# Activations as the loaded weights: FFNs, output projections and cross output of a three-layer block in f32 products, with the residual stream turned to tokens on the partitions

## Chip, cores and metric

One core of one Trainium2 chip. Times are device microseconds of a whole execution; lower is better. A matmul here has a stationary operand (128x128, put in by an instruction of its own, the weight load) and a moving operand, whose columns stream through.

## What is computed

x is 256 tokens by 2048 features, all in f32. Two layers:

```python
h = rms_norm(x, norm1_g[l])
q, k, v, gu, gv = split(h @ w_in[l])            # 2048 x 3584
attn = banded_window_attention(rope(norm(q)), rope(norm(k)), v, sink)
sgu  = chunked_spatial_gating(gelu(gu), gelu(gv), ...)
x = x + concat(rms_norm(attn), rms_norm(sgu)) @ w_o[l]        # 2048 x 2048
a = depthwise_conv(rms_norm(x) @ w_up[l])       # 2048 x 11264, three taps along the tokens
x = x + (silu(a_gate) * a_up) @ w_down[l]       # 5632 x 2048
```

Then one layer of another kind: a mixer of dilated attention and a state-space scan (input 2048 x 6160, output `w_out` 2048 x 2048), cross attention to 256 memory tokens (`w_ckv`, `w_cq`, and the output `w_co`, 512 x 2048), and an FFN `relu(h @ w_up)**2 @ w_down` with 8192 hidden features. Each part reads an rms norm of x and adds to x.

## The kernel before

All weight matrices are cut into 560 pieces of 1 MB (128 partitions x 2048 numbers) in the order of use. For each piece SP issues the load into one of four slots `w_raw`, as soon as TensorE has finished the piece four before (`acc_done`); ACT rounds it to the format fp32r (`w_hi`, L1031), DVE subtracts (`w_lo`, L1462, in place of `w_raw`), both two pieces ahead of TensorE (`tick(p, s)` splits piece p + 2). Every product is three fp32r matmuls: hi x hi, hi x lo, lo x hi. ACT, DVE and TensorE each run the pieces in the written order, with their other work placed between `tick`s by hand; a later operation waits for all before it on its engine.

Features lie on the partitions everywhere. The residual stream `xs` is [16 chunks of 128 features, 256 tokens]. Weights are the stationary operand, activations move, 256 columns (tokens) at a time, 48 matmuls a piece. `wide` makes 128 output features from all 2048 inputs (L456 to L458), `deep` 512 output features from 512 inputs (L473 to L475), `mixed_half` one half of an output projection (L516 to L518), because the two halves have their own rms factor and the factors are applied after the product, per column (token), by DVE (`add_mixed`). `evac_scaled` takes a finished bank out of PSUM times the token factor (L1491), `evac_deep` adds a down piece to `xs` (L1497, two additions of 128x512).

An FFN block of the layers is 8 up pieces (512 gate and 512 up features) and the 4 down pieces of the block before. For each pair of up pieces: ACT makes the base of the convolution (L1206), DVE adds two taps (L1695, L1696), ACT the silu (L1210), DVE the product (L1714), ACT `h_hi` (L1212), DVE `h_lo` (L1716). A loop runs over five pairs of blocks. The second FFN has 16 blocks of 4 up and 4 down pieces.

The inputs of a projection are x times the norm's gain, split in hi (ACT, L1034) and lo (DVE, L1479); the rms factor comes later. Its sum of squares: POOL squares x in eight steps and sums (L360, L362), TensorE sums over the partitions with a matrix of ones (`total_pairs`, L489), ACT and DVE make the inverse root over 128x256 (`inverse_root`). At the start x comes in one transposed load of four parts, `wdt` (the 16 step columns of the mixer) with the constants; DVE waits for the constants ahead of w_lo of piece 2.

Of the kernel before, what the change touches and what calls it, by code (L numbers as in the profile page):

```python
# [15 lines left out]
P = 128  # L40
# [62 lines left out]
LAYER_LINKS = 159  # L103
NORMS = 7
SQUARED, SUMMED = 24, 20
# [3 lines left out]
def build(nc, x, weights, wdt, params1, params2, consts, consts1, w_s, b_s, mem, positions, out):  # L109
    ctx = ExitStack()  # L110
    with ctx:
# [16 lines left out]
        xs = fixed("x_stream", [KC, T])  # L128
# [20 lines left out]
        wdt_sb = fixed("wdt_sb", [KC, SSM_HEADS])  # L149
# [13 lines left out]
        ff = at("ff_tmp", [6, T], F32, AA)  # L163
        gr, ur, ga, ua, gs, hm = (ff[:, i] for i in range(6))
# [22 lines left out]
        sums2 = at("factored", [2, T], F32, AA + 8 * KB)  # L187
# [20 lines left out]
        sq_x = at("sq_x", [KC, T], F32, AR + 16 * KB)  # L208
# [22 lines left out]
        def psb(a, n):  # L231
# [19 lines left out]
        first_squares = sem("first_squares")  # L251
# [30 lines left out]
        wdt_ready, dt_sums, softplus_in, softplus_out, dt_rows = (  # L282
            sem(n) for n in ("wdt_ready", "dt_sums", "softplus_in", "softplus_out", "dt_rows"))
# [35 lines left out]
        @block.sync  # L319
        def _(sp):  # L320
            x_parts = x.rearrange("(c p) t -> p c t", p=P)
            for s in range(W_SLOTS):
                if s == 1:
                    for j in range(4):
                        sp.dma_start(xs[:, 4 * j:4 * j + 4], x_parts[:, 4 * j:4 * j + 4]).then_inc(x_in[j], 16)
                sp.dma_start(w_raw[:, s], weights[s]).then_inc(raw_in[s], 16)
            with sp.Fori(1, PIECES // W_SLOTS) as i:
# [6 lines left out]
            y = out.rearrange("(c p) t -> p c t", p=P)  # L334
            for j in range(DOWN):
                sp.wait_ge(acc_free, PIECES - DOWN + j + 1 + 4)
                sp.dma_start(y[:, 4 * j:4 * j + 4], xs[:, 4 * j:4 * j + 4]).then_inc(out_done, 16)
            sp.wait_ge(out_done, 16 * DOWN)
# [3 lines left out]
        def _(pool):  # L342
# [5 lines left out]
            pool.dma_start(wdt_sb[:], wdt).then_inc(consts_in, 16)  # L348
# [17 lines left out]
            for i in range(7):  # L366
                pool.wait_ge(first_squares, (i + 1) // 2 + 1)
                if i:
                    pool.wait_ge(x_summed, i)
                G.tensor_tensor(sqa[:], sqa[:] if i else sq_x[:, 0:2], sq_x[:, 2 * i + 2:2 * i + 4],  # L370
                                ALU.add).then_inc(x_summed, 1)
            pool.wait_ge(consts_in, 4 * 16)
            with pool.Fori(0, LAYERS) as l:
                P0, N0, SQ0, SU0 = l * LAYER_PIECES, l * NORMS, l * SQUARED, l * SUMMED + 7

                pool.wait_ge(acc_free, P0 + 4)
# [4 lines left out]
                pool.wait_ge(sums_ready, N0 + 3)  # L381
# [16 lines left out]
                for i in range(4):  # L398
                    pool.wait_ge(gated, 2 * l + (1 if i < 3 else 2))
                    add_squares(SQ0 + 4, SU0 + 3, i, proj[:, U1 + 2 * i:U1 + 2 * i + 2], N0 + 4)  # L400

                for i in range(8):
                    pool.wait_ge(acc_free, P0 + P_OUT + (2 * i + 2 + 4))
                    add_squares(SQ0 + 8, SU0 + 6, i, xs[:, 2 * i:2 * i + 2], N0 + 5)

                for i in range(8):
                    pool.wait_ge(acc_free, P0 + (LAYER_PIECES - DOWN + i // 2 + 1 + 4))
                    add_squares(SQ0 + 16, SU0 + 13, i, xs[:, 2 * i:2 * i + 2], N0 + 6)
            N0, SQ0, SU0 = LAYERS * NORMS, LAYERS * SQUARED, LAYERS * SUMMED + 7

            pool.wait_ge(acc_free, P_IN2 + 4)
            pool.dma_start(pos_sb[:], positions.to_broadcast([P, T])).then_inc(positions_in, 16)
            pool.wait_ge(gains_ready, 2 * LAYERS + 2)
            pool.wait_ge(sums_ready, N0 + 3)
# [3 lines left out]
            for n in range(4):  # L418
                pool.wait_ge(heads_copied, LAYERS * 2 + n + 1)
                add_squares(SQ0, SU0, n, proj[:, Q2 + 2 * n:Q2 + 2 * n + 2], N0)  # L420
# [9 lines left out]
            for i in range(8):  # L430
                add_squares(SQ0 + 4, SU0 + 3, i, mem_sb[:, 2 * i:2 * i + 2], N0 + 3)
            pool.wait_ge(acc_free, 4 + P_KV)
            for i in range(8):
                add_squares(SQ0 + 12, SU0 + 10, i, xs[:, 2 * i:2 * i + 2], N0 + 5)
            for i in range(8):
                pool.wait_ge(acc_free, P_CO + i // 2 + 1 + 4)
                add_squares(SQ0 + 20, SU0 + 17, i, xs[:, 2 * i:2 * i + 2], N0 + 6)
# [3 lines left out]
        def _(pe):  # L441
# [4 lines left out]
            def wide(p, s, acts, free=1, ready=None):  # L446
# [3 lines left out]
                pe.wait_ge(acc_free, p + free)  # L450
                o = ps[:, s, 0:T]
                for c in range(KC):
# [6 lines left out]
                last.then_inc(acc_done, 1)  # L459


            FREE = (3, 2, 2, 1)

            def deep(p, s, hi_in, lo_in):
# [11 lines left out]
                last.then_inc(acc_done, 1)  # L476
# [14 lines left out]

            def per_head(n, o, sq, chunks, per_row=1, base=K_SEL):
# [11 lines left out]
            def mixed_half(p, s, half, ready=None):  # L504

                if half == 0:
                    pe.wait_ge(w_ready, p + 1)
                    pe.wait_ge(acc_free, p + 1)
                o = ps[:, s, half * T:(half + 1) * T]
                src_hi, src_lo = (act_hi, act_lo) if half else (mix_hi, mix_lo)  # L510
                for i in range(8):
                    c = 8 * half + i
                    hi, lo = w_hi[:, s, c * P:(c + 1) * P], w_lo[:, s, c * P:(c + 1) * P]
                    if ready is not None:
                        pe.wait_ge(act_ready, ready + c + 1)
                    mm(o, hi, src_hi[:, i], start=i == 0, stop=False)  # L516
                    mm(o, hi, src_lo[:, i], start=False, stop=False)  # L517
                    last = mm(o, lo, src_hi[:, i], start=False, stop=i == 7)  # L518
                if half:
                    last.then_inc(acc_done, 1)  # L520
# [38 lines left out]
            with pe.Fori(0, LAYERS) as l:  # L559
                P0, N0, S0, A0, SU0 = l * LAYER_PIECES, l * NORMS, l * 2, l * PREPS, l * SUMMED + 7  # L560

# [1670 lines left out]
```

## Time and profile before

| what | value |
|---|---|
| median of 3 runs | 3573.75 us (3571.2 to 3575.15) |
| the profiled execution, first to last instruction | 3573.6 us |
| TensorE matmuls | 3485.6 us busy, 27974 records |
| TensorE weight loads | 3415.4 us busy, 27974 |
| DVE, ACT, POOL busy | 2339.1, 1532.4, 284.6 us |
| read from memory | 594.54 MB, 167 GB/s over the span |
| mean granted clock of TensorE | 0.983 |

Matmuls overlap, so a busy TensorE is not one at its peak: the distance between starts says more than the busy time. A plain f32 matmul leaves two records, an fp32r matmul or a transpose one. The profiled execution has only its span (3573.6); it lies at the median of the runs.

### The profile page before, as it was taken

How to read it: one execution, taken by the hardware profiler on the slowest of the kernel's cores; microseconds unless marked ns; L12 is line 12 of the kernel's file. 1: busy time of each engine (PE TensorE's matmuls, PEld its weight loads, DVE VectorE, ACT ScalarE, POOL GpSimd, SP SyncE). 2: the span in 40 equal slices, each digit the busy share in tenths (PEclk: the TensorE clock that was granted, in tenths of full speed). 3: DMA queues.
4: the chain of work that ended last, by engine and by line, in shares of the span. 5: the costliest groups of instructions: out<-in, count | busy, mean ns of one | idle time of the engine just before them, and what ended most of it. 6: DMA issues, size and time to landing. Idle time of an engine off the chain costs nothing.

```text
span 3573.6 us, 67331 instructions
## 1 busy us (share of the span) xinstructions
PE 3485.6 (98%) x27974; PEld 3415.4 (96%) x27974; DVE 2339.1 (65%) x2609; ACT 1532.4 (43%) x1578; POOL 284.6 (8%) x177
## 2 busy tenths in 40 slices
PE   8999999999999999999999999999999899999999
PEld 8999999999998989999999999989898899999999
DVE  5658666666667658766666668467777756555555
ACT  4554434443443454444344344337643433333332
POOL 1113000000003013000000002010032200000000
PEclk9999999999999999999999999999999999999999
DMA  6335545555554424545454454433354355554544
GB/s 225 131 112 182 181 177 182 174 187 177 177 179 160 152 107 175 179 179 177 176 187 175 181 177 156 165 129 136 126 184 146 130 178 187 177 187 177 187 177 165
DMA packets 86527, 600.05 MB, mean 168 GB/s; under 512 B 9328, under 2 KB 13456, under 8 KB 14624
## 3 DMA queue, kind: packets, MB, share of 16 engines
q1 hardware_dynamic: 84864, 591.43, 46.2%
q0 software_dynamic: 1440, 5.24, 0.5%
q8 instruction: 189, 3.10, 0.3%
q14 instruction: 34, 0.28, 0.0%
HBM read 594.54 MB, written 2.10 MB: 167 GB/s over the span
## 4 chain that ended last, share of the span: by engine, by line
PE 85%; DVE 6%; issue 4%; ACT 2%; POOL 2%; DMA 1%; DVEq 0%; SPq 0%; ACTq 0%; POOLq 0%
PE ps L456 18%; PE ps L457 18%; PE ps L458 18%; PE ps L473 8%; PE ps L475 8%; PE ps L474 8%; DVE act_lo L1479 1%; POOL squares L360 1%; DVE w_lo L1462 1%; PE ps L516 1%; PE ps L518 1%; PE ps L517 1%; DVE actb_lo L1479 1%; DVE x_stream L1497 1%; DMA w_raw<-in_weights 1%
## 5 line engine op out<-in xcount | busy, mean ns | idle before, releaser
L1031 ACT ACTIVATE w_hi<-w_raw 128x2048 fp32r<-128x2048 f32 x560 | 1064.1, 1905 | 639.1 <-DMA w_raw<-in_weights 638.3
L1462 DVE TENSOR_TENSOR w_lo<-w_raw,w_hi 128x2048 fp32r<-128x2048 f32 x560 | 1286.2, 2298 | 73.4 <-ACT w_hi L1031 64.4
L456 PE MATMUL ps<-actb_hi,w_hi 128*128 128x256 f32 x3968 | 1129.3, 285 | 21.5 <-DVE x_stream L1497 13.9
L457 PE MATMUL ps<-actb_lo,w_hi 128*128 128x256 f32 x3968 | 1126.9, 284 | 6.5 <-issue 6.5
L458 PE MATMUL ps<-actb_hi,w_lo 128*128 128x256 f32 x3968 | 1126.3, 284 | 0.0
L456 PEld LDWEIGHTS ps<-actb_hi,w_hi 128*128 128x128 f32 x3968 | 765.3, 193 | 24.7 <-DVE x_stream L1497 15.4
L457 PEld LDWEIGHTS ps<-actb_lo,w_hi 128*128 128x128 f32 x3968 | 765.5, 193 | 7.8 <-issue 7.6
L458 PEld LDWEIGHTS ps<-actb_hi,w_lo 128*128 128x128 f32 x3968 | 765.3, 193 | 0.0
L473 PE MATMUL ps<-h_hi,w_hi 128*128 128x256 f32 x2432 | 688.3, 283 | 0.0
L474 PE MATMUL ps<-h_lo,w_hi 128*128 128x256 f32 x2432 | 688.3, 283 | 0.0
L475 PE MATMUL ps<-h_hi,w_lo 128*128 128x256 f32 x2432 | 688.2, 283 | 0.0
L456 PE MATMUL ps<-act_hi,w_hi 128*128 128x256 f32 x1728 | 510.2, 295 | 38.3 <-DVE act_lo L1479 20.7
L457 PE MATMUL ps<-act_lo,w_hi 128*128 128x256 f32 x1728 | 498.7, 289 | 0.0
L458 PE MATMUL ps<-act_hi,w_lo 128*128 128x256 f32 x1728 | 498.3, 288 | 0.0
L474 PEld LDWEIGHTS ps<-h_lo,w_hi 128*128 128x128 f32 x2432 | 466.9, 192 | 0.0
L475 PEld LDWEIGHTS ps<-h_hi,w_lo 128*128 128x128 f32 x2432 | 466.9, 192 | 0.0
L473 PEld LDWEIGHTS ps<-h_hi,w_hi 128*128 128x128 f32 x2432 | 466.9, 192 | 0.0
L1497 DVE TENSOR_TENSOR x_stream<-x_stream,ps 128x512 f32<-128x512 f32 x312 | 200.4, 683 | 307.4 <-PE ps L475 307.4
L456 PEld LDWEIGHTS ps<-act_hi,w_hi 128*128 128x128 f32 x1728 | 342.0, 198 | 50.1 <-DVE act_lo L1479 22.6
L1491 DVE TENSOR_TENSOR ff_tmp<-ps,factors 128x256 f32<-128x256 f32 x240 | 101.9, 424 | 379.8 <-PE ps L458 379.8
L457 PEld LDWEIGHTS ps<-act_lo,w_hi 128*128 128x128 f32 x1728 | 342.3, 198 | 2.3 <-issue 2.0
L458 PEld LDWEIGHTS ps<-act_hi,w_lo 128*128 128x128 f32 x1728 | 341.6, 198 | 0.0
(283 smaller groups left out, 3222.5 us busy)
## 6 DMA issues: line engine op xcount, KB each, us to landing
w_raw<-in_weights SPq DMA_DIRECT2D x560, 1024.0 KB, 4.8
x_stream<-in_x SPq DMA_DIRECT2D x4, 512.0 KB, 8.8
mem_sb<-in_mem POOLq DMA_DIRECT2D x4, 512.0 KB, 6.5
out_xT<-x_stream SPq DMA_DIRECT2D x4, 512.0 KB, 3.0
w_s_sb<-in_w_s POOLq DMA_DIRECT2D x2, 512.0 KB, 4.5
consts_sb<-in_consts POOLq DMA_DIRECT2D x1, 686.5 KB, 8.7
consts_sb<-in_consts POOLq DMA_DIRECT2D x1, 576.0 KB, 10.8
params_sb<-in_params POOLq DMA_DIRECT2D x1, 434.0 KB, 7.4
```

The source lines that it names most:

```text
L360: G.tensor_tensor(sqt[:], src, src, ALU.mult).then_inc(x_squared, 1)
L456: mm(o, hi, acts[0][:, c], start=c == 0, stop=False)
L457: mm(o, hi, acts[1][:, c], start=False, stop=False)
L458: last = mm(o, lo, acts[0][:, c], start=False, stop=c == KC - 1)
L473: mm(o, hi, hi_in[:, c], start=c == 0, stop=False)
L474: mm(o, hi, lo_in[:, c], start=False, stop=False)
L475: last = mm(o, lo, hi_in[:, c], start=False, stop=c == 3)
L1031: A(w_hi[:, s], w_raw[:, s], ACT.Identity).then_inc(hi_done, 1)
L1462: tt(w_lo[:, s], w_raw[:, s], hi_of(w_hi[:, s]), ALU.subtract).then_inc(w_ready, 1)
L1479: stt(dst[1][:, c], src(c), gains(c), hi_of(dst[0][:, c]), ALU.mult, ALU.subtract).then_inc(act_ready, 1)
L1491: tt(dst, ps[:, s, 0:T], factors, ALU.mult).then_inc(acc_free, 1)
L1497: last = tt(dst, dst, psb(2 * (s % 2) + j, 2), ALU.add)
```

## The change

In the FFNs, the output projections (`w_o`, `w_out`) and the cross output, the activations become the stationary operand (128 features x 128 tokens) and 512 columns of the weights move. The products stay the same three; a piece takes 24 matmuls, and what comes out has tokens on the partitions, 2 x 128 x 512. The pieces of these matrices are laid out anew (`token_pieces`: 512 inputs by 512 outputs); their number and size stay. `wide` stays for `w_in`, the mixer's input, and the cross q, k, v.

- `xs` is [2 blocks of 128 tokens, 2048 features]; the kernel is given x both ways (4 MB in place of 2), and the output leaves token-major.
- The two halves of an output projection are 8 pieces each, one after the other, and each is added with its factor per partition (`add_scaled`).
- Ahead of each norm x is turned by TensorE into PSUM, a quarter (8 transposes of 128x128) behind each finished quarter (`x_quarter`); ACT and DVE make hi and lo from there (`x_hi`, `x_lo`). Squares and their sums come from ACT (`x_squared`, accumulated along the features), not from POOL and TensorE; the inverse root is over 2 columns. Where a factor is still needed per column, a diagonal matrix and ones make a row of it (`factor_row`). A layer's first three pieces run interleaved by quarters of x (`opening`).
- The convolution runs along the tokens, so an up half of 512 features is copied out of PSUM (ACT, with the factor), turned (8 transposes) and convolved by four features' chunks at once. In the second FFN the relu is copied and turned likewise, then squared by ACT.
- `evac_deep` becomes one addition of 128x1024. Accumulators of up and down pieces are two banks each; TensorE waits for `added` of two pieces before.
- `dt_products` uses the hi and lo inputs in place of `xs` (32 products in place of 16); `wdt` is loaded ahead of the mixer, not at the start.
- The two layers are written out; the inner loop runs over four pairs of FFN blocks, the first and the last block stand outside.

```diff
@@ TensorE
+            def tokens(p, s, acts, c0, bank, first=True, last=True):
                 pe.wait_ge(w_ready, p + 1)
-                pe.wait_ge(acc_free, p + 3)
-                for j in range(4):
-                    o = ps[:, 2 * (s % 2) + j // 2, j % 2 * T:(j % 2 + 1) * T]
+                for b in range(TB):
+                    o = ps[:, bank + b, :]
                     for c in range(4):
-                        cols = slice(c * 512 + j * P, c * 512 + (j + 1) * P)
-                        hi, lo = w_hi[:, s, cols], w_lo[:, s, cols]
-                        mm(o, hi, hi_in[:, c], start=c == 0, stop=False)
-                        mm(o, hi, lo_in[:, c], start=False, stop=False)
-                        last = mm(o, lo, hi_in[:, c], start=False, stop=c == 3)
-                last.then_inc(acc_done, 1)
+                        a_hi, a_lo = (a[:, c0 + c, b * P:(b + 1) * P] for a in acts)
+                        hi, lo = w_hi[:, s, c * 512:(c + 1) * 512], w_lo[:, s, c * 512:(c + 1) * 512]
+                        mm(o, a_hi, hi, start=first and c == 0, stop=False)
+                        mm(o, a_lo, hi, start=False, stop=False)
+                        end = mm(o, a_hi, lo, start=False, stop=last and c == 3)
+                end.then_inc(acc_done, 1)
+            def turned(bank, src, j):
+                for c in range(4):
+                    for b in range(TB):
+                        end = nc.tensor.transpose(ps[:, bank + c // 2, c % 2 * T + b * P:c % 2 * T + (b + 1) * P],
+                                                  src[:, b, j * 512 + c * P:j * 512 + (c + 1) * P], ident)
+                return end
+            def x_quarter(j, sums, ready):
+                pe.wait_ge(added, sums)
+                pe.wait_ge(act_ready, ready)
+                turned(4 + 2 * (j % 2), xs, j).then_inc(x_turned, 1)
+            def opening(p, w, ready, sums=None, turn=None):
+                for s in range(3):
+                    if sums is not None and s == 0:
+                        pe.wait_ge(added, sums - 1)
+                    elif sums is not None and s == 2:
+                        turn()
+                    wide(p + s, w + s, s, A_IN, ready if s == 0 else None, range(8))
+                for part in range(8, KC, 4):
+                    for s in range(3):
+                        wide(p + s, w + s, s, A_IN, ready if s == 0 else None, range(part, part + 4))
...
+                def step(b, par, first=False):
+                    p = F0 + UP1 + (b - 1) * (UP1 + DOWN)
+                    for half in range(2):
+                        pe.wait_ge(added, D1 + 4 * (b - 2) + 3 + half)
+                        for q in range(4):
+                            tokens(p + 4 * half + q, q, B_IN, 4 * q, 2 * half, q == 0, q == 3)
+                            if half == 0 and q == 0 and first:
+                                turned_up(b - 1, 1)
+                            elif half == 1 and q == 0:
+                                pe.wait_ge(conv_done, U0 + 2 * b - 1)
+                                turned_up(b, 0)
+                    pe.wait_ge(h_split, H0 + b)
+                    for j in range(DOWN):
+                        pe.wait_ge(added, D1 + 4 * (b - 1) + j - 1)
+                        tokens(p + UP1 + j, j, (h_hi[:, 1 - par], h_lo[:, 1 - par]), 0, 2 * (j % 2))
+                        if j == 0:
+                            pe.wait_ge(conv_done, U0 + 2 * b)
+                            turned_up(b, 1)
...
             def dt_products():
-                pe.wait_ge(wdt_ready, 1)
-                for c in range(KC):
-                    last = mm(ps[0:16, 6, 0:T], wdt_sb[:, c], xs[:, c], start=c == 0, stop=c == KC - 1)
+                pe.wait_ge(wdt_in, 16)
+                for part, acts in enumerate(A_IN):
+                    for c in range(KC):
+                        last = mm(ps[0:16, 6, 0:T], wdt_sb[:, c], acts[:, c].bitcast(F32),
+                                  start=part == 0 and c == 0, stop=part == 1 and c == KC - 1)
@@ DVE
-            def evac_deep(p, s):
-                dve.wait_ge(acc_done, p + 1)
-                for j in range(2):
-                    dst = xs[:, 4 * s + 2 * j:4 * s + 2 * j + 2]
-                    last = tt(dst, dst, psb(2 * (s % 2) + j, 2), ALU.add)
-                last.then_inc(acc_free, 1)
+            def add_plain(p, j):
+                dve.wait_ge(acc_done, p + 1)
+                dst, bank = xs[:, :, 512 * j:512 * j + 512], 2 * (j % 2)
+                tt(dst, dst, ps[:, bank:bank + 2, :], ALU.add).then_inc(added, 1)
...
+                def taps(b, half):
+                    dst, bank = (ga, ua)[half], 4 + 2 * half
+                    src = lambda c, t: ps[:, bank + c // 2, c % 2 * T + t:c % 2 * T + t + T - 1]
+                    for c in range(4):
+                        if c % 2 == 0:
+                            dve.wait_ge(conv_base, 2 * U0 + 4 * b + 2 * half + c // 2 + 1)
+                        last = stt(dst[:, c, 1:T], src(c, 0), col(b, c, half, 0), dst[:, c, 1:T], ALU.mult, ALU.add)
+                    step(last)
+                    for c in range(4):
+                        last = stt(dst[:, c, 0:T - 1], src(c, 1), col(b, c, half, 2), dst[:, c, 0:T - 1], ALU.mult, ALU.add)
+                    last.then_inc(conv_done, 1)
...
+                def step1(b, par, first=False):
+                    p = F0 + UP1 + (b - 1) * (UP1 + DOWN)
+                    for k in range(UP1):
+                        tick(p + k, k % 4)
...
+                        elif k == 5:
+                            taps(b, 0)
+                    for k in range(DOWN):
+                        add_plain(p + UP1 + k, k)
+                        tick(p + UP1 + k, k)
+                        if k == 1:
+                            taps(b, 1)
+                            gated_hidden(b)
+                        elif k == 2:
+                            hidden_lo(b, par)
```

## Rows read from the trace of the kernel before

**Rows 1.** The page: busy time, chain by engine, one group of section 5

```profile
PE 3485.6 (98%) x27974; PEld 3415.4 (96%) x27974; DVE 2339.1 (65%) x2609; ACT 1532.4 (43%) x1578; POOL 284.6 (8%) x177
...
PE 85%; DVE 6%; issue 4%; ACT 2%; POOL 2%; DMA 1%; DVEq 0%; SPq 0%; ACTq 0%; POOLq 0%
...
L1031 ACT ACTIVATE w_hi<-w_raw 128x2048 fp32r<-128x2048 f32 x560 | 1064.1, 1905 | 639.1 <-DMA w_raw<-in_weights 638.3
```

**Rows 2.** Timeline, TensorE in an FFN block: start us, length us, instruction

```profile
799.99 0.28 PE L474 MATMUL ps<-h_lo,w_hi 128*128 128x256 f32 x1
...
801.19 0.28 PE L475 MATMUL ps<-h_hi,w_lo 128*128 128x256 f32 x1
```

**Rows 3.** Windows: span; busy (x instructions) PE, PEld, DVE, ACT, POOL; PEclk, DMA share, GB/s

```profile
345.00:1105.00 760.00, 750.52 (x6219) 749.30 (x6218) 498.94 (x575) 323.76 (x315) 7.76 (x4) 1.00 0.51 179
2845.00:3569.00 724.00, 723.92 (x6033) 723.72 (x6032) 427.59 (x441) 255.69 (x187) 0.00 (x0) 1.00 0.50 180
```

**Rows 4.** Waits of TensorE over the whole span: total us, times, longest

```profile
PE ps L456 <- DVE x_stream L1497: 13.9, 8, 2.0
PE ps L457 <- issue: 6.5, 5, 1.7
```

**Rows 5.** A window behind one wait in the FFN of layer 0

```profile
524.00:528.00 4.00, 4.00 (x23) 4.00 (x22) 0.40 (x1) 0.00 (x0) 0.00 (x0) 0.58 0.33 135
```

**Rows 6.** Windows: start, a probabilities stage, three joints

```profile
1105.00:1140.00 35.00, 27.36 (x185) 26.16 (x184) 28.88 (x21) 14.61 (x15) 19.18 (x14) 0.85 0.38 137
...
2712.00:2740.00 28.00, 21.85 (x153) 20.12 (x153) 26.32 (x30) 8.40 (x9) 9.49 (x8) 0.88 0.32 113
2785.00:2845.00 60.00, 48.68 (x330) 46.12 (x329) 46.87 (x41) 23.83 (x27) 25.67 (x15) 0.89 0.30 105
...
10.00:60.00 50.00, 43.61 (x319) 43.11 (x320) 29.73 (x39) 27.19 (x29) 15.40 (x13) 0.93 0.63 235
154.00:163.00 9.00, 9.00 (x79) 9.00 (x78) 5.37 (x6) 8.97 (x21) 0.00 (x0) 1.00 0.49 182
```

**Rows 7.** Timeline, TensorE's first matmuls at the start

```profile
11.27 0.41 PE L456 MATMUL ps<-act_hi,w_hi 128*128 128x256 f32 x1
...
11.91 0.41 PE L456 MATMUL ps<-act_hi,w_hi 128*128 128x256 f32 x1
```

**Rows 8.** Timeline, plain f32 records of 512 columns

```profile
111.84 3.60 PE L597 MATMUL ps<-arena,rot_gains 128*128 128x512 f32 x8
```

**Rows 9.** Timeline, loads of 128 columns with matmuls of two

```profile
2334.76 3.63 PE L752 MATMUL ps<-consts_sb,sq_q 128*128 128x2 f32 x32
```

**Rows 10.** Timeline, a lot of transposes and the stream behind it

```profile
156.72 1.91 PE L553 MATMUL ps<-consts_sb,scores_h 128*128 128x128 f32 x16
...
158.59 0.28 PE L457 MATMUL ps<-act_lo,w_hi 128*128 128x256 f32 x1
```

**Rows 11.** Timeline, DVE: the operations nearest to the new ones

```profile
657.18 1.28 DVE L1497 TENSOR_TENSOR x_stream<-x_stream,ps 128x512 f32<-128x512 f32 x2 [2.27 <-PE ps L475]
658.38 2.28 DVE L1462 TENSOR_TENSOR w_lo<-w_raw,w_hi 128x2048 fp32r<-128x2048 f32 x1
...
130.45 3.23 DVE L1510 SCALAR_TENSOR_TENSOR scores_h<-ps,query_factors,consts_sb 128x256 f32<-128x256 f32 x8 [0.83 <-PE ps L542]
...
602.82 0.48 DVE L1696 SCALAR_TENSOR_TENSOR ff_tmp<-ff_tmp,params_sb 128x255 f32<-128x255 f32 x1 [0.22 <-DVE ff_tmp L1695]
...
2785.53 1.23 DVE L2039 COPY vt<-ps 128x1024 f32<-128x1024 f32 x1
```

**Rows 12.** The page, DMA issues: KB each, us from issue to landing

```profile
w_raw<-in_weights SPq DMA_DIRECT2D x560, 1024.0 KB, 4.8
```

**Rows 13.** Timeline, the start: ACT, DVE, TensorE

```profile
17.44 3.88 ACT L1082 ACTIVATE sq_x<-x_stream 128x1024 f32<-128x1024 f32 x4
...
28.23 7.77 DVE L1462 TENSOR_TENSOR w_lo<-w_raw,w_hi 128x2048 fp32r<-128x2048 f32 x3 [8.38 <-DMA wdt_sb<-in_wdt]
...
30.58 0.58 PE L456 MATMUL ps<-act_hi,w_hi 128*128 128x256 f32 x1 [4.65 <-DVE w_lo L1462]
```

More of the change, by code:

```diff
@@ L489, in total_pairs, with token_sums @@
                     last = mm(ps[:, bank, 0:T], ones, sqa[:, c], start=c == 0, stop=c == 1)
+                last.then_inc(sums_ready, 1)
+            def token_sums(bank, summed):
+                pe.wait_ge(x_summed, summed)
+                for b in range(TB):
+                    for c in range(2):
+                        last = mm(ps[:, bank, b:b + 1], sqa[:, c, b * P:(b + 1) * P], ones[:, 0:1],
+                                  start=c == 0, stop=c == 1)
                 last.then_inc(sums_ready, 1)
@@ L502, in per_head, with mixed @@
                 last.then_inc(sums_ready, 1)
[L504 to L513, printed above, removed]
-                    if ready is not None:
[L515 to L520, printed above, removed]
+            def mixed(p, group, acts, ready=None):
+                for q in range(2):
+                    if ready is not None:
+                        pe.wait_ge(act_ready, ready + 4 * q + 4)
+                    tokens(p + q, (p + q) % W_SLOTS, acts, 4 * q, 2 * (group % 2), q == 0, q == 1)
             def spread(r, bank, rows):
@@ new lines, in _ @@
+                for half in range(2):
+                    pe.wait_ge(added, D1 - 1 + half)
+                    for q in range(4):
+                        if half == 0:
+                            pe.wait_ge(act_ready, A0 + 2 * KC + 4 * q + 4)
+                        tokens(F0 + 4 * half + q, q, B_IN, 4 * q, 2 * half, q == 0, q == 3)
+                        if q == 0 and half == 0:
+                            x_quarter(3, D1, A0 + 2 * KC + 8)
+                        elif q == 0:
+                            turned_up(0, 0)
@@ new lines, in _ @@
+                x_hi(X0, 3, actb_hi, ffn_gain)
+                x_root_of(2 * l + 1)
+                tick(F0 + 2, 2)
+                tick(F0 + 3, 3)
+                act.wait_ge(x_factors, 2 * l + 2)
+                copy(0, 0, F0 + 4)
+                for k in range(4, UP1):
+                    tick(F0 + k, k % 4)
+                    if k == 5:
+                        base(0, 0)
+                    elif k == 6:
+                        silu(0)
+                copy(0, 1, F0 + 8)
+                step1(1, 1, True)
@@ new lines, in step2 @@
+            def step2(b, par, first=False):
+                p = P_FF2 + UP2 + (b - 1) * (UP2 + DOWN)
+                for k in range(UP2 + DOWN):
+                    tick(p + k, k % 4)
+                    if first and k == 1:
+                        hidden2(b - 1, 1 - par)
+                    elif k == 3:
+                        copy2(b, p + 4, 4)
+                    elif k == 5:
+                        hidden2(b, par)
+            tick(P_FF2 + 2, 2)
+            tick(P_FF2 + 3, 3)
+            act.wait_ge(x_factors, 7)
@@ new lines, in _ @@
+                tick(F0, 0)
+                tick(F0 + 1, 1)
+                x_mean(2 * l + 1)
+                x_lo(A0 + 2 * KC, 3, B_IN, ffn_gain)
+                x_inverse(2 * l + 1)
+                for k in range(2, UP1):
+                    tick(F0 + k, k % 4)
+                    if k == 5:
+                        taps(0, 0)
+                step1(1, 1, True)
+                with step.loop((BLOCKS1 - 3) // 2, 4) as i:
+                    step1(2 * i + 2, 0)
+                    step1(2 * i + 3, 1)
```

1008 lines of the change are left out of this document (553 added, 455 removed).

## Prediction

> **What bounds the kernel now.** I read the page's busy table first, then the costliest groups, then windows by stage, and last the single rows from which a duration comes. TensorE is busy 98% of the span, and the chain that ended last runs 85% over matmuls of the weight stream [rows 1]. So only time on TensorE counts, and everything else counts where TensorE waits for it.
>
> How full is TensorE really? In the stream the starts of ten consecutive matmuls lie 1.20 us apart, 0.120 us each [rows 2]; a piece of weights is 48 of them, 5.76 us. The second FFN holds 6033 matmuls in 724.0 us: at 0.120 that is 723.7 (two or three of the count straddle an edge), so nothing is lost there. The FFN of one layer holds 6219 in 760: 746 accounted for, 14 lost [rows 3]. The waits name the cause, 13.9 us over eight waits for DVE's addition `L1497` in the two layers, and 6.5 us of issue [rows 4]; part of the rest is half clock (0.58 after one such wait) [rows 5]. Like this, each f32 record at its own spacing, the joints give their loss: 13.0 us at the end of layer 0 (layer 1 alike), 8.8 before the cross queries, 18.8 from the cross values to the second FFN [rows 6]; some 4 of these lie in the cross attention, which stays. The 560 pieces are 26,880 matmuls x 0.120 = 3226 us of 3573.6.
>
> **What a matmul of 256 columns pays for.** 0.120 us is not streaming alone. At half clock the same pair of load and matmul takes 0.213 us (0.64 for three) [rows 7]: 256 columns at 1.2 GHz are 213.3 ns, one column per clock with nothing on top. At 2.4 GHz the columns would need 106.7 ns; 13 are missing. Plain f32 records of 512 columns come every 0.43 us with a weight load each (eight in 3.60, the last one's 0.59 included) [rows 8], two clocks a column (0.4267) and 3 ns on top. So a fixed price shows only when the stream is short. Loads of 128 columns of weights with matmuls of only two columns come every 0.112 us (32 in 3.63) [rows 9]. So the weight load, 0.112 or a little more in this format, is what a 256-column matmul at full clock waits for.
>
> **Part 1, the matmuls that change shape.** 444 of 560 pieces (2 x 16 output, 264 FFN pieces in the layers, 16 second output, 4 cross output, 128 second FFN) go from 48 matmuls of 256 columns to 24 of 512. No row of before shows one in this format. Lower bound: 512 at one per clock, 0.213. Upper bounds: the 13 ns stay, 0.227; or the 0.120 belongs to the columns, 0.240. I take 0.216, one column per clock and the 3 ns of [rows 8], its nearest row. Gain: 444 x 24 = 10,656 matmuls x (0.240 - 0.216) = **-255.7 us** (bounds -284, -142, 0).
>
> The Trainium skill ("TensorE: Matmul & The Clock Gate", Back-to-back issue gap) gives for a warm matmul N/2.4 + 2.5 ns. It agrees on 512 columns (215.8) but says 109.2 for 256, where the rows show 120. By the Trainium skill alone, two short ones would cost 218.4 and the change would gain 2.6 ns x 10,656 = 28 us, less than its transposes cost; an estimate from that page of the Trainium skill, which the measured 120 overrules.
>
> **Part 2, the transposes it adds.** f32 transposes of 128x128: 16 in 1.75 us, from 156.72 to the next stream matmul, whose successor starts at 158.59 [rows 10], so 0.109 each and no price for changing over. FFN of the layers: 22 blocks x 16; second FFN: 16 x 8; the residual stream, turned six times x 32. 672 x 0.109 = **+73.2**.
>
> **Part 3, small sums.** `dt_products` goes from 16 to 32 f32 products of two records each (0.215 a record of 256 columns, half of [rows 8]): +6.9. Twelve `total_pairs` go (four records, 0.86 each, -10.4); `token_sums` (40 short records at 0.112) and four rows of factors (0.43) come, +6.2. **+2.7**.
>
> **Part 4, the FFN loop in the layers.** Who is late? Take the downs of a block, PE done with down 1 at time 0. DVE then does, in program order: addition (128x1024, 1.23 long; next start 1.14 later), w_lo of down 3 (2.20), `taps` for the up half (eight operations at 0.40 with a wait of 0.22 between the fours: 3.5), `gated_hidden` (0.2 + 1.14), the addition of down 2 (1.14), w_lo of the next piece (2.28): with semaphores 11.7 us [rows 11]. PE arrives after downs 2 and 3, 2 x 24 x 0.216 = 10.4. PE waits **1.4 us in each of blocks 1 to 9**. After block 10 it wants the split hidden values too (1.2 more): 2.6. Per layer 15.2, plus the issue waits that stay (3.3): 18.5 against 14.1 now, since the two-us waits at the loop's turn go (there the next up waited for all additions; now only for down 2's). **+9**. Bounds: no stall, -30 (DVE only a little quicker); 3 us a block, +32.
> Elsewhere in the block DVE and ACT have room: DVE 12 x 2.3 + 16 x 0.4 + 6 x 1.2 = 41 of 65 us; ACT 12 x 1.9, four copies, eight bases, silu and h_hi, some 32. In the second FFN hidden_lo follows w_lo, DVE is done 1.7 us ahead: no stall. New waits: PE waits for ACT's copies before it turns an up half (behind it stand the next pieces), but the copy (two of 128x512, under 1.3 us) ends during the piece issued between them (5.2); on ACT the copy waits for PE with a w_hi queued behind it, whose piece runs two pieces later. Transfers: a slot comes free three pieces (15.5 us) ahead; landing 4.8, w_hi 1.9, w_lo 2.3 are 9.0 [rows 1, 11, 12]. 1 MB in 5.2 us is 202 GB/s; the window at the start moved 235 [rows 6].
>
> **Part 5, the joints.** Layer end: a quarter of x is turned right behind each down, and the next layer opens with three pieces interleaved by quarters. DVE reaches the second quarter's low part 3.5 us (addition, w_lo) behind the last down; PE has turned quarter 2 (0.87) and four chunks (1.4) until then, and waits 1.7, perhaps with some half clock: 2.5. Of 13.1 that saves 10.6, twice: -21. Cross output to second FFN: the first four chunks now last a whole piece (5.2) and cover the rest: -14. Cross queries: x_quarter runs under the last K pieces, -7.8. Second output: 41 us of first-half work cover y where 12 did; no row here shows a loss there, so I count nothing. Start: ahead of w_hi of piece 2, ACT now waits for 2 MB more (token-major x; 8.5 us at the window's 235 GB/s, part of it under w_hi of piece 1) and makes eight squares with sums of half the size instead of four (3.88), say 6. PE waits 4.65 us there already, for DVE, which waits for `wdt`; that load is now moved [rows 13]. +6 (bounds 0 and +12). **-37**. On POOL's queue `wdt` now goes out at layer 1's end, ahead of `positions`; 128 KB, where a piece of 1 MB lands in 4.8 us, have four pieces (23 us) until `dt_products`. POOL's squares of x vanish; they were off the path.
>
> **Sum.** -255.7 + 73.2 + 2.7 + 9 - 37 = -208. The execution profiled has a span of 3573.6 us, the median of the runs is 3573.75. So **3366 us**.
>
> **Rivals.**
> *The 13 ns stay* (0.227 at 512): it is a swap of weights, not a load that sticks out. The half-clock row, with nothing on top, and the 3 ns of the f32 rows speak against it. 3366 + 10,656 x 0.0107 = 3480.
> *DVE's order costs more in the FFN*: the longer wait also lowers the clock, or `taps` out of PSUM beside two writers is slower. 2.5 us more a block x 20: 3416. For it: one of the eight waits of about 2 us is followed by half clock [rows 5], and there are to be twenty; against it, mine are shorter.
> *The lots of transposes lower the clock*: the FFNs have 60 lots of eight, and a stretch like that of [rows 5] (0.58 over 4 us) costs 1.7 us: 3366 + 102 = 3468 at most. Against it: the 16 transposes at 156.72 stand in a window at clock 1.00 [rows 6, 10].
> *Slower than before*: the price is by column. If the moving side reads this format at 256 columns in 0.120 us, whatever is loaded, 512 take 0.240 and the transposes come on top: 3366 + 255.7 = 3622. From 0.2355 us a matmul up it decides (3573.6 - 3366 = 208, over 10,656, on top of 0.216). For it: each matmul record is 0.28 us long whatever stands around it [rows 2], as if the engine itself took the 0.120. Against it: half clock shows 0.213, not 0.240 or more. (Taking the Trainium skill's 2.6 ns a pair off the measured 0.240 would give 3594, on this side too; it shares this chance.)
> That the change might not do what it says I can exclude: counts and shapes stand in the code.
>
> **How the numbers follow.** My case 0.78, own range 3335 to 3400 (0.2133 a matmul, or no FFN stall, below; +30 from stalls above). The 13 ns 0.07, DVE 0.07, clock 0.03, slower 0.05. Range 3325 to 3420 takes in my case and DVE's and leaves out about 0.18: the 13 ns, slower, clock, and the tails of mine. Faster by over 0.2% (about what a measurement of this kernel can tell from no change) 0.94, within 0.01 (a price near 0.2355), slower 0.05.
>
> **What would show it.** Starts of the 512-column matmuls 0.216 apart; a piece at 5.2 us; lots of 8 transposes of 0.87; one wait of 1.4 us for w_lo per FFN block, at its first up; the stretch that held the second FFN's 6033 matmuls down from 724 to 664 us (126 pieces x 0.576 less, 128 transposes more, no wait); the joints down to 2 or 3 us. Wrong would be: 0.227 or 0.240, or DVE's wait at other places.

## The result, and the profile after

The changed kernel takes 3451.57 us (median of four runs, 3449.5 to 3452.47) against 3573.61 for the kernel before in the same comparison: ratio 0.9655, 95% interval 0.9642 to 0.9669. Faster, but by 122 us and not by the 208 forecast; 3366 was wrong, and the range ended 32 us below the result. The profiled execution has a span of 3449.7 us, 123.9 less than before.

The page, busy shares, the share of the chain by engine and line, and some groups (busy us, mean ns of one, idle before it and its releaser):

```profile
PE 3395.1 (98%) x18022; PEld 2900.8 (84%) x18022; DVE 2049.6 (59%) x1888; ACT 1617.2 (47%) x1640; POOL 111.5 (3%) x80
...
L473 PE MATMUL ps<-w_hi,actb_hi 128*128 128x512 f32 x1920 | 751.5, 391 | 12.1 <-DVE w_lo L1615 12.1
...
L441 PE MATMUL ps<-act_hi,w_hi 128*128 128x256 f32 x1728 | 503.6, 291 | 24.2 <-DVE w_lo L1615 10.6
...
L473 PEld LDWEIGHTS ps<-w_hi,actb_hi 128*128 128x128 f32 x1920 | 360.5, 188 | 93.0 <-DVE w_lo L1615 17.3
```

TensorE stays at 98% of the span, with 18,022 matmuls where 27,974 were; so the time per instruction went up, and the next view must say to what. Timeline of TensorE in an FFN block, eleven starts on end:

```profile
799.68 0.39 PE L473 MATMUL ps<-w_hi,actb_hi 128*128 128x512 f32 x1
...
801.72 0.39 PE L473 MATMUL ps<-w_hi,actb_hi 128*128 128x512 f32 x1
801.95 0.39 PE L474 MATMUL ps<-w_hi,actb_lo 128*128 128x512 f32 x1
```

From 799.68 to 801.95 are ten spacings, 2.27 us: 0.227 each, not the 0.216 of the forecast. Over the whole trace 10,082 of 10,572 spacings between two such matmuls are 226 or 227 ns (mean 226.7), and the 256-column ones still stand 120 apart, as in [rows 2]. The second FFN, which had nothing to hide in before either [rows 3], gives the same in one window:

```profile
2745.00:3445.00 700.00, 700.00 (x3155) 581.08 (x3153) 373.69 (x209) 287.17 (x188) 0.00 (x0) 1.00 0.52 187
```

It holds 3025 matmuls of 512 columns and 128 transposes: 3025 x 0.2267 + 128 x 0.109 = 699.7 of 700. (A further two records of the 3155 straddle its edges.)

TensorE's waits, then the same by window for the stages of [rows 3] and [rows 6] (span; busy and instructions of PE, PEld, DVE, ACT, POOL; PEclk, DMA share, GB/s):

```profile
PE ps L473 <- DVE w_lo L1615: 12.3, 19, 0.8
PE ps L441 <- DVE w_lo L1615: 10.6, 6, 6.9
PE ps L441 <- DVE act_lo L1632: 10.4, 1, 10.4
PE ps L473 <- DVE h_lo L1895: 3.2, 2, 1.6
PE ps L441 <- DVE act_lo L1643: 3.2, 2, 1.6
```

```profile
10.00:60.00 50.00, 41.50 (x312) 41.07 (x313) 26.65 (x42) 27.26 (x39) 2.64 (x5) 0.93 0.70 268
331.00:1083.00 752.00, 744.32 (x3379) 615.47 (x3377) 450.75 (x394) 352.35 (x317) 0.00 (x0) 1.00 0.52 184
1070.00:1095.00 25.00, 23.39 (x154) 21.19 (x153) 20.72 (x26) 18.66 (x34) 1.10 (x2) 1.00 0.40 148
```

The waits stand where the forecast put them. Eighteen of the nineteen waits for `w_lo` stand at the first up piece of the FFN blocks (the last, 0.2 us, at the second output); two of 1.6 us after the tenth block, for `h_lo`; two of 1.6 us at the layer ends, for the third quarter's low part. Only the spacing of a 512-column matmul is another. The issue waits of [rows 4] are gone.

To see what belongs to what, I take each record of TensorE at its own spacing (0.120 and 0.2267 in the stream, 0.109 for a transpose, two clocks a column for plain f32) and call the rest lost. Before 135.7 us are lost, after 78.1, 57.7 less; the own spacings fall by 66.1, where 142.1 - 73.2 - 2.7 is 66.2. Part of what is no longer lost is clock: its mean rises from 0.983 to 0.991. As an estimate, 0.017 x 3573.6 = 61 us of full clock were missing before and 0.009 x 3449.7 = 31 are after; not all of it counts, since TensorE also waits at half clock. The forecast had this only as "perhaps with some half clock".

### The profile page after: what moved, and what is told of

It is laid out like the page before. It is cut to its first block, busy times and chain, and to the rows that moved or that the text cites. A ratio compares the mean times of both kernels' runs of the same rounds, so it can differ in the third digit from the quotient of the medians.

```text
span 3449.7 us, 44217 instructions
## 1 busy us (share of the span) xinstructions
PE 3395.1 (98%) x18022; PEld 2900.8 (84%) x18022; DVE 2049.6 (59%) x1888; ACT 1617.2 (47%) x1640; POOL 111.5 (3%) x80
## 4 chain that ended last, share of the span: by engine, by line
PE 87%; DVE 9%; issue 1%; ACT 1%; DMA 1%; DVEq 0%; SPq 0%; ACTq 0%
PE ps L473 21%; PE ps L475 21%; PE ps L474 21%; PE ps L441 6%; PE ps L442 5%; PE ps L443 5%; DVE w_lo L1615 4%; PE ps L482 2%; DVE x_stream L1695 1%; DVE up_conv L1882 1%; DVE up_conv L1885 1%; PE ps L662 1%; PE ps L661 1%; DMA x_stream<-in_x 0%; PE ps L565 0%
## 5 line engine op out<-in xcount | busy, mean ns | idle before, releaser
L473 PE MATMUL ps<-w_hi,actb_hi 128*128 128x512 f32 x1920 | 751.5, 391 | 12.1 <-DVE w_lo L1615 12.1
L474 PE MATMUL ps<-w_hi,actb_lo 128*128 128x512 f32 x1920 | 747.3, 389 | 0.0
L475 PE MATMUL ps<-w_lo,actb_hi 128*128 128x512 f32 x1920 | 747.3, 389 | 0.0
L473 PE MATMUL ps<-w_hi,h_hi 128*128 128x512 f32 x1216 | 476.6, 392 | 3.2 <-DVE h_lo L1895 3.2
L475 PE MATMUL ps<-w_lo,h_hi 128*128 128x512 f32 x1216 | 473.3, 389 | 0.0
L474 PE MATMUL ps<-w_hi,h_lo 128*128 128x512 f32 x1216 | 473.3, 389 | 0.0
L473 PEld LDWEIGHTS ps<-w_hi,actb_hi 128*128 128x128 f32 x1920 | 360.5, 188 | 93.0 <-DVE w_lo L1615 17.3
L475 PEld LDWEIGHTS ps<-w_lo,actb_hi 128*128 128x128 f32 x1920 | 360.5, 188 | 75.1
L474 PEld LDWEIGHTS ps<-w_hi,actb_lo 128*128 128x128 f32 x1920 | 360.6, 188 | 73.3
L441 PEld LDWEIGHTS ps<-act_hi,w_hi 128*128 128x128 f32 x1728 | 336.4, 195 | 33.8 <-DVE w_lo L1615 22.4
L473 PEld LDWEIGHTS ps<-w_hi,h_hi 128*128 128x128 f32 x1216 | 228.4, 188 | 50.1 <-DVE h_lo L1895 4.1
L474 PEld LDWEIGHTS ps<-w_hi,h_lo 128*128 128x128 f32 x1216 | 228.5, 188 | 45.9
## 6 DMA issues: line engine op xcount, KB each, us to landing
consts_sb<-in_consts POOLq DMA_DIRECT2D x1, 576.0 KB, 12.1
```

The costliest lines, as they stand in the source:

```text
L441: mm(o, hi, acts[0][:, c], start=c == 0, stop=False)
L473: mm(o, a_hi, hi, start=first and c == 0, stop=False)
L474: mm(o, a_lo, hi, start=False, stop=False)
L475: end = mm(o, a_hi, lo, start=False, stop=last and c == 3)
```

## The experiments

### What the 13 ns go with: TensorE by itself

A kernel with nothing but matmuls on rounded x, 48 of each shape on a line of its own:

```
            # b: 384 columns
            for i in range(N):
                mm(ps[:, bank(i), 0:384], st[:, i % 16], mv[:, i % 4, 0:384], **flags(i))
            ...
            # f: 256 columns, 64 stationary columns
            for i in range(N):
                mm(ps[0:64, bank(i), 0:256], st[:, i % 16, 0:64], mv[:, i % 4, 0:256], **flags(i))
```

> Leaves the whole computation out: TensorE alone multiplies rounded x by rounded x in 13 stretches of 48 matmuls, each of another shape, after 72 matmuls of warm-up, and x itself is written out. What is disputed is the 13.3 ns that each fp32r matmul of the changed kernel shows on top of its columns at full clock. Theory A, a fixed part of every fp32r matmul, whatever is loaded: 512 columns 226.7 ns, 384 columns 173.3, 256 columns 120.0, and the same three figures when the loaded weights stay the same, have 64 columns or 64 rows, or when nothing is accumulated. Theory B, an exchange of the loaded weights, which grows with their columns: 64 loaded columns take about 6.7 ns less (220.0 at 512 columns, 113.3 at 256), and the same weights again up to 13.3 less (213.3). The step of my forecast, a weight load that sticks out from under 256 columns: 512 columns 213 to 216 ns, and 256 columns fall below 120 with 64 loaded columns. Of bf16 and plain float32 none of the three says anything; bf16 at 213 to 216 for 512 columns would tie the 13.3 ns to the format.

Its timeline, the first record of each shape and the first of the next shape (a lot's length is from one start to the next start, by 48):

```profile
33.81 0.39 PE L65 MATMUL ps<-move_r,still_r 128*128 128x512 f32 x1
...
44.69 0.69 PE L68 MATMUL ps<-move_r,still_r 128*128 128x384 f32 x3
...
53.04 0.28 PE L71 MATMUL ps<-move_r,still_r 128*128 128x256 f32 x1
...
58.78 0.40 PE L74 MATMUL ps<-move_r,still_r 128*128 128x512 f32 x1
...
69.69 0.40 PE L77 MATMUL ps<-move_r,still_r 128*64 128x512 f32 x1
...
80.73 0.28 PE L80 MATMUL ps<-move_r,still_r 128*64 128x256 f32 x1
...
86.18 0.40 PE L83 MATMUL ps<-move_r,still_r 128*128 128x512 f32 x1
...
97.09 0.61 PE L86 MATMUL ps<-move_b,still_b 128*128 128x512 bf16 x2
...
107.46 0.27 PE L89 MATMUL ps<-move_b,still_b 128*128 128x256 bf16 x1
...
112.70 0.59 PE L92 MATMUL ps<-x_plain 128*128 128x512 f32 x1
```

In fp32r: 512 columns 10.88 / 48 = 226.7 ns, 384 columns 8.35 / 48 = 174.0 (most spacings 173 or 174), 256 columns 5.74 / 48 = 119.6 (most spacings 120). One line through all three: a column per clock (0.4167 ns) and 13.3 ns on top. The same weights again (`L74`) 227.3, nothing accumulated (`L83`) 227.3; with 64 rows 41 of 48 spacings are 226 or 227. In bf16: 512 columns 216.0, 256 columns 109.2, that is 2.7 and 2.5 on top. Plain f32 keeps the figures of [rows 8], 429.2 a record of 512 columns.

So the step of the forecast falls: with 64 loaded columns (`L80`) the load is shorter, 134 ns long where it was 188, and the spacing at 256 columns goes only to 113.5, not to the 106.7 of the bare columns; and at 512 columns, where a load has 213 ns to hide in, the price is still there. The 13 ns belong to the format. With 64 loaded columns they halve at 256 columns (theory B's figure), but at 512 columns they rise (`L77`, 230.0). That fits neither theory.

> Leaves the whole computation out, as the first of its kind: TensorE alone, 48 matmuls of each shape, to see what the 13.3 ns of an fp32r matmul go with. In the first one 64 loaded columns took 113.3 ns at 256 columns, but 230 in the mean at 512; the same weights again took 226.7. Theory B, a price for exchanging the loaded weights that goes with their columns (0.104 ns a column): at 256 columns 120.0, 116.7, 113.3 and 110.0 ns for 128, 96, 64 and 32 loaded columns; at 320 and 192 columns with 128 loaded 146.7 and 93.3; at 128 and 64 columns the load itself is longer than the matmul and sets the time. bf16 with 64 loaded columns: 107.9 if its 2.5 ns go with the columns too, 109.2 if they are fixed. Theory A, a fixed price in which 64 loaded columns are an exception: 120.0 for 96 and 32 as well. At 512 columns the exception is still open: 220 for 64 by theory B, 230 measured; 96 and 32 show whether it is a pattern.

With the same kernel form, mean spacings in ns:

```
loaded columns      128     96      64      32
256 moving          119.8   116.0   113.5   113.4
512 moving          226.7   230.0   230.0   231.6   (128 and 64: first kernel)
moving columns, 128 loaded: 320 -> 146.6, 192 -> 111.2, 128 -> 111.0
```

At 320 columns the line holds (133.3 + 13.3 = 146.7). At 192 it doesn't (93.3 expected): there the load itself sets 111, the figure of [rows 9] at a format where I had it "or a little more". Theory B's series, 116.7 and 113.3, is met for 96 and 64, not for 32 (110.0), and at 512 columns fewer loaded columns cost more. A price that is proportional to the loaded columns is thereby out, a price that is independent of them as well. What remains shown is the rule for 128 loaded columns at full clock, which is all that these kernels use. The lots with 64 moving columns and with bf16 and 64 loaded ran partly at half clock (granted clock 0.59 and 0.77), so their means say nothing, but their single spacings do. In bf16 those at full clock are 109 or 110: the 2.5 ns do not go with the loaded columns. With 64 moving columns they are 111 or 112 at full clock and 213 or 214 at half: there the load sets the time at either clock. So half clock at 256 columns, 213, cannot tell the load from the columns; only 512 columns can. In bf16 the load is quicker: 128 moving and 128 loaded columns come every 55.5 ns, with loads 98 ns long where those in fp32r are 188 to 192. Whether the 13.3 ns come from the format's slower load, from an exchange of the weights or from the matmul stays open. A matmul without its load, which would separate them, was not tried: the lot with the same weights again has 48 loads, too.

### A third of the change taken back: 256-column matmuls in the downs

```
-                for b in range(TB):
-                    o = ps[:, bank + b, :]
+                halves = ((0, 256), (256, 512)) if first and last else ((0, 512),)
+                for b, (n0, n1) in ((b, h) for b in range(TB) for h in halves):
+                    o = ps[:, bank + b, n0:n1]
...
-                        hi, lo = w_hi[:, s, c * 512:(c + 1) * 512], w_lo[:, s, c * 512:(c + 1) * 512]
+                        hi, lo = (w[:, s, c * 512 + n0:c * 512 + n1] for w in (w_hi, w_lo))
```

> The changed kernel with every 512-column matmul of the down projections and the cross output made as two of 256 columns: 3,744 matmuls more, the same columns. A fixed 13.3 ns for each matmul: 3,744 x 0.0133 = +50 us on the changed kernel, about 3501 us (3497 to 3506), and each of the halves at 120.0 ns. If the 13.3 ns went with columns and not with the matmul, the time stays at 3452. If a 256-column matmul is held up by its weight load beyond what a 512-column one is, it is over +55 us.

3528.38 us, +76.8: by its size the third, a 256-column matmul held up by its load. The spacings say otherwise, 120 in 11,852 of 12,915 pairs of 256 columns. By spacings the matmuls account for +49.9; the loss rises by 28.5 (78.1 to 106.5). The waits name it:

```profile
PE ps L474 <- issue: 16.7, 9, 3.2
PE ps L476 <- issue: 13.2, 3, 4.5
```

Twelve waits that nothing in the profile releases, 29.9 us; the six longest pairs stand every two blocks, once per turn of the FFN loops, and five of them are followed by 6.8 or 10.2 us at half clock. The changed kernel has none. Six stretches of 50 to 80 us, one around each pair, lose 44 us together. The rise is smaller because the waits for `w_lo` at the first up pieces, which cost the changed kernel about 15, are gone: a TensorE that is slower in the downs comes to them later. The instruction queue moved 160 packets here, 95 in the changed kernel, 189 in the kernel before, which has 6.5 us of issue [rows 4]. This points to the fetching of the loop's code at its turn, but I did not test that apart, and the number of instructions alone does not explain it: the kernel before has more matmuls in a turn of its loop (1152 against 768 in this version) and loses less to issue. 49.9 + 28.5 = 78.4 is the difference of the spans (3528.1 and 3449.7). So the price of a matmul is 13.3 ns in the kernel too; the issue waits were missing in my expectation.

### The transposes doubled

```
-                for c in range(4):
+                for c in (0, 1, 2, 3, 0, 1, 2, 3):
```

It stands in the helper `turned`, so each of the 672 transposes is made twice, those of the residual stream too (the expectation names the hidden pieces alone; its count is of all).

> The changed kernel with each transpose of the hidden pieces made twice, 672 transposes more of 128 columns. At the 109 ns that my forecast took for one, with PE on the path throughout: +73 us, about 3525 us (3515 to 3532). If they ran under other work, or cost their columns alone (53 ns each): +36 or less, below 3490.

3522.26 us, +70.7. In the spans +67.7: +73.4 by count, and 5.8 us less loss. The FFN waits for `w_lo` have no part in that: they stay at 12.1 us in 18. At each layer end 0.9 us less is lost, and 3.2 us less in two stages of the last layer in which the changed kernel runs partly at half clock (see "The layer ends without the interleaving"). The mean clock stays at 0.991. The term of +73.2 stands, and the rival that lots of transposes lower the clock is out.

### DVE's order in the FFN

`gated_hidden` and the splits of the hidden values one down piece later, in all blocks but the last (on ACT `hidden_hi` in the same way); on the vector engine

```
                         if k == 1:
                             taps(b, 1)
+                        if k == (1 if last else 2):
                             gated_hidden(b)
-                        elif k == 2:
+                        if k == (2 if last else 3):
                             hidden_lo(b, par)
```

> The changed kernel with one edit: the vector and scalar operations that prepare the next block's hidden pieces stand behind the addition of one more down piece, in all FFN blocks but the last. The wait of PE at the first up piece of each block (12.3 us in 19 waits, 0.85 us lost at each of 18) should go: -15 us, about 3436 us (3433 to 3442). Rival: the pieces then come late for the down matmuls that load them, and PE waits there as long: 3450 to 3456.

3432.68 us, ratio to the kernel before 0.9602 (0.9586 to 0.9618): 18.9 us less than the changed kernel, and 17.5 less loss, 17.6 of it in the FFNs of the two layers, where the edit is. In the changed kernel DVE's timeline between down 1 and the next up piece is

```profile
501.53 1.22 DVE L1695 TENSOR_TENSOR x_stream<-x_stream,ps 128x1024 f32<-128x1024 f32 x1 [2.91 <-PE ps L475]
502.67 2.29 DVE L1615 TENSOR_TENSOR w_lo<-w_raw,w_hi 128x2048 fp32r<-128x2048 f32 x1
504.87 1.65 DVE L1882 SCALAR_TENSOR_TENSOR up_conv<-ps,params_sb,up_conv 128x255 f32<-128x255 f32 x4
506.66 1.65 DVE L1885 SCALAR_TENSOR_TENSOR up_conv<-ps,params_sb,up_conv 128x255 f32<-128x255 f32 x4
508.44 1.23 DVE L1891 TENSOR_TENSOR hidden<-gate_silu,up_conv 128x1024 f32<-128x1024 f32 x1
509.58 1.22 DVE L1695 TENSOR_TENSOR x_stream<-x_stream,ps 128x1024 f32<-128x1024 f32 x1
510.71 2.29 DVE L1615 TENSOR_TENSOR w_lo<-w_raw,w_hi 128x2048 fp32r<-128x2048 f32 x1
```

with TensorE waiting at the end of it,

```profile
513.06 0.50 PE L473 MATMUL ps<-w_hi,actb_hi 128*128 128x512 f32 x1 [0.68 <-DVE w_lo L1615]
```

and with the new order `hidden` no longer stands ahead of the addition and of `w_lo`:

```profile
510.26 1.21 DVE L1695 TENSOR_TENSOR x_stream<-x_stream,ps 128x1024 f32<-128x1024 f32 x1
511.38 2.29 DVE L1615 TENSOR_TENSOR w_lo<-w_raw,w_hi 128x2048 fp32r<-128x2048 f32 x1
513.59 1.22 DVE L1891 TENSOR_TENSOR hidden<-gate_silu,up_conv 128x1024 f32<-128x1024 f32 x1
```

The waits of `L473` for `w_lo` are gone from the list; the two for `h_lo` stay.

### The layer ends without the interleaving

```
-                for s in range(3):
-                    ...
-                    wide(p + s, w + s, s, A_IN, ready if s == 0 else None, range(8))
-                for part in range(8, KC, 4):
-                    ...
+                pe.wait_ge(added, sums - 1)
+                wide(p, w, 0, A_IN, ready, range(8))
+                turn()
+                wide(p, w, 0, A_IN, ready, range(8, KC))
+                wide(p + 1, w + 1, 1, A_IN)
+                wide(p + 2, w + 2, 2, A_IN)
```

> The changed kernel with the first three pieces after each layer's end one after the other, as the kernel before had them, and not interleaved by quarters: what the interleaving is worth at the two ends. My theory: PE has 24 matmuls instead of 72 between the last down piece and the first that needs the third quarter of the residual stream, so it waits some 4 to 7 us more at each of the two ends: +8 to +14 on 3452, about 3462. Rival, the turned quarters come in time anyway and the joint saved because of the smaller sums: 3451 to 3454.

3457.16 us, +5.6, between my +8 and the rival's nothing. At each of the two ends

```profile
PE ps L441 <- DVE act_lo L1640: 5.0, 3, 2.2
```

stands where 1.6 us in one wait stood: 3.4 more. The loss in these two windows of 50 us rises by 4.5 and 5.9, 10.4 in all and within my +8 to +14; part of it is half clock behind the waits. 5.6 of it comes back elsewhere, and most of that not by this edit: between 2240 and 2320 us and between 2680 and 2730 us the granted clock is 0.94 and 1.00 here, 0.91 and 0.97 in the changed kernel; by estimate 0.03 x 80 + 0.03 x 50 = 3.9 us of full clock. The version with the later start has the 0.94 in the first of these windows too, with nothing changed there. So interleaving is worth about 5 us at each end, and a difference of 2 to 4 us between two versions' whole times can be such a shift of the clock in a stage that neither edit touches.

### The start

```
-                if s == 1:
+                if s == 2:
                     sp.dma_start(xs[:], x.rearrange("(b p) d -> p b d", p=P)).then_inc(x_tokens_in, 16)
```

and the squares of x on ACT moved behind the splits of pieces 2 and 3.

> The changed kernel with the load of x in token order one piece of weights later, and the squares of x on the scalar engine behind the splits of pieces 2 and 3. My theory of the start: of the 6.9 us that PE waits for w_lo of piece 2, most is the scalar engine's wait for that load and its squares: -5 to -7, about 3446. Rival, the wait is for the vector engine or the weights themselves: 3450 to 3453.

3454.08 us (3451.01 to 3456.57): no gain. My theory of the start falls. TensorE's waits in the first 60 us, with the edit:

```profile
PE ps L462 <- DVE newton L1662: 5.0, 1, 5.0
PE ps L441 <- DVE w_lo L1614: 4.9, 2, 3.9
```

The wait for `w_lo` of piece 2 goes from 6.9 to 3.9 us, since DVE, no longer behind ACT's squares, waits for the load of the parameters instead, as it waited for a load before the change [rows 13]; and the token factors, later now, hold up the factor row for 5.0. The start's window (10 to 60 us) loses 16.2 us where it lost 12.1. From 10 to 35 us the DMA engines are busy for 0.99 of the time in the changed kernel and for 1.00 with the edit, at 398 and 400 GB/s (322 before the change). My reading is that the start is bound by what these transfers bring and that an edit of order only chooses which wait shows; a start with fewer bytes was not run.

> The changed kernel with both edits, the order of the FFN's vector operations and the start. The first alone measured 3432.7. If the two add up: 3426 to 3429, 0.960 of the kernel before; if the start gains nothing, 3432.

3434.65 us, ratio 0.9606 (0.9593 to 0.9619): no better than the order alone. The best version is the changed kernel with the new order of DVE's operations.

## Why the prediction was wrong, step by step

Spans: 3573.6 to 3449.7 are -123.9. The parts: -142.1 + 73.2 + 2.7 - 57.7 = -123.9.

**What a matmul of 256 columns pays for (wrong).** This is the step that failed: "the weight load, 0.112 or a little more in this format, is what a 256-column matmul at full clock waits for". What is paid is a price of the fp32r matmul with 128 loaded columns, 13.3 ns, and it stays at 512 columns, where a load of 0.112 has 0.213 to hide in. What inside the engine it pays for is open. I had two rows for my reading, and both show less than I took from them. At half clock 213 is the time of 256 columns and, as the lot with 64 moving columns shows, that of the load as well. Half clock with nothing on top [rows 7] shows in the changed kernel at 512 columns as well, at full clock 13.3 ns notwithstanding:

```profile
2709.42 0.63 PE L473 MATMUL ps<-w_hi,act_hi 128*128 128x512 f32 x1
...
2710.27 0.63 PE L475 MATMUL ps<-w_lo,act_hi 128*128 128x512 f32 x1
```

(Two spacings in 0.85 us; the records stand 426 or 427 ns apart, which is 512 columns at 1.2 GHz.) The price shows at one clock and not at the other, so its absence at half clock says nothing on whether it is fixed. And the 3 ns of [rows 8] are those of another format, which bf16 shares.

**Part 1.** Its count was right, its price not: 10,656 x 0.0133 = 142.1 us where 255.7 stood. I took the row nearest in length (512 columns, plain f32) over the one nearest in format (256 columns, fp32r). The other reading was written down as the bound 0.227 and as the rival at 3480, with a chance of 0.07, too little, and the range ended below it.

**The rule weighed.** The Trainium skill ("TensorE: Matmul & The Clock Gate", Back-to-back issue gap) gives N/2.4 + 2.5 ns. The bf16 rows agree (216.0 and 109.2), plain f32 as well if its two clocks a column are put in for N/2.4 (429.2 a record of 512 columns); the fp32r rows of 512 and 256 columns do not (226.7 and 119.6). That the measured 120 overruled it was right. But I let its 215.8 and the plain f32 row confirm each other at 512 columns, where neither had seen the format.

**Part 2, right.** The transposes stand at 0.109, and doubled they cost 73.4 by count, 67.7 in the spans.

**Part 3.** Not tested by itself; it is in the own spacings, whose sum closes within 0.1.

**Part 4, mechanism right, its size 15 us off.** Every wait is at the piece forecast, and the chain on DVE takes 11.5 us (501.53 to 513.0) where 11.7 was worked out. TensorE comes at 2 x 24 x 0.2267 = 10.9 and not at 10.4, so a block loses 0.85 and not 1.4; after block 10 1.8 instead of 2.6; and the 3.3 us of issue per layer that I kept are gone. The FFNs of the layers lose 22.4 us (28.2 before) where I had 37. The wrong price made this term too dear: a slower matmul hides more.

**Part 5, right within some microseconds.** Layer ends 13.1 and 13.2 to 2.0 each, -22.3 (forecast -21). From the second output to the second FFN 31.7 to 6.8, -24.9 (-21.8). Start +1.1 (+6): the squares wait as forecast, but DVE would have waited for the parameters anyway. Another -5.8 came in the stages that I counted as unchanged.

With 0.2267 in the place of 0.216 the forecast would have been 3366 + 113.6 = 3480 (3479.4 as a span), and the span measured, 3449.7, is 29.7 below that: -14.6 for the FFNs, -1.3 the layer ends, -3.1 the cross part, -4.9 the start, -5.8 the rest. These terms happened to lean the other way; without them the forecast would have been further off still.

**The other rivals.** Slower by a price by column: out, 0.2267 and not 0.240. DVE's order costs more: out, it cost less. Transposes lower the clock: out.

What the change is worth, piece by piece: 24 matmuls fewer give 0.32 us. An up piece of the FFNs pays two transposes for it, 0.22, and keeps 0.10; a down piece keeps all. The turning of the residual stream (192 transposes, 21 us) is less than the 47.2 us that the layer ends and the cross part save.

## What to carry to other kernels

Where the new shape of a matmul isn't in the trace, take its price from the rows of the same format, not from rows of the same columns in another format or at another clock, and let the range hold both readings of a gap when they differ by half of the gain. When the engine on the path turns out slower per piece, the waits for the engines behind it shrink, so correct the two together. The order of a helper engine's work between the last pieces of a loop's turn deserves a run of its own; here it gave 19 us for a few moved lines. And when an edit acts in one stage, read its worth from the loss in that stage as well as from the whole time.

## What the runs showed of the hardware

- An fp32r matmul with 128 loaded columns takes a column per clock and 13.3 ns at full clock (120, 146.6, 174, 226.7 ns at 256, 320, 384 and 512 columns), nothing on top at half clock (213, 427), and not under 111 ns (192, 128 and 64 columns; 213 at half clock for 64). bf16 and plain f32 records have 2.2 to 2.8 ns on top at full clock; bf16 goes down to 55.5 ns at 128 columns.
- Loading fewer columns helps at 256 moving columns (116.0, 113.5 and 113.4 ns for 96, 64 and 32 loaded) and doesn't at 512: 230.0 to 231.6 ns. Why is open.
- The version with 3,744 matmuls more has 29.9 us of issue waits, at the turns of the FFN loops, five of the six pairs with half clock behind them; the changed kernel has none. The cause was not tested, and the kernel before, with more matmuls in a turn, has 6.5.
